# Hybrid decoder step on one core: who copies turned pages and probabilities, where swish stands, and the order of loads in the output projection

## The reference, cut to what matters

```
z = rmsnorm(x) @ w_in                       # q, k, v, indexer q and k, conv inputs
attention: each query attends to its top 256 keys by an indexer's score
   prompt: causal over 1024 rows; sample: 2048 cached rows (16 pages) + 8 new ones
convolution branch: GLU -> depthwise conv (31) -> layernorm -> c * sigmoid(c)
m = concat(attention, conv) @ w_out ;  x = x + rmsnorm(m)
x = x + rmsnorm( relu(rmsnorm(x) @ w_up)^2 @ w_down )
```

## Time and profile before

| | us |
|---|---|
| median of 3 runs | 1666.31 |
| lowest, highest | 1664.51, 1667.41 |
| the profiled execution | 1657.09 |
| its span | 1655.3 |
| TensorE busy in the span | 1534.6 (93%) |
| VectorE, ScalarE, GpSimd busy | 692.7, 605.1, 434.5 |

### The profile page before, as it was taken

One profiled execution on the slowest core, in us unless ns is written; L12 is line 12 of the kernel. 1 busy time (PEld: TensorE's weight loads), 2 busy tenths in 40 slices (PEclk: granted clock), 3 DMA queues, 4 the chain that ended last, 5 costly groups with the idle time before them and its releaser, 6 DMA issues.

```text
span 1655.3 us, 22168 instructions
## 1 busy us (share of the span) xinstructions
PE 1534.6 (93%) x8544; PEld 1278.0 (77%) x8544; DVE 692.7 (42%) x1318; ACT 605.1 (37%) x1084; POOL 434.5 (26%) x445
## 2 busy tenths in 40 slices
PE   4798898998969999888999999999999999999995
PEld 2356625663468877456879999999999999999995
DVE  1234916788977545243554222222222222222234
ACT  3112725988425764474443121121212112130211
POOL 2132100112595321341433121212121212122224
PEclk8999998999989998998999999999999999999998
DMA  6010104142106100544001111111111111111112
GB/s 209 20 36 24 52 2 128 60 69 55 19 1 185 54 2 1 216 166 147 0 1 55 48 39 51 38 51 39 50 38 51 38 51 38 51 38 51 39 49 98
DMA packets 92884, 97.66 MB, mean 59 GB/s; under 512 B 14822, under 2 KB 80438, under 8 KB 90500
## 3 DMA queue, kind: packets, MB, share of 16 engines
q1 hardware_dynamic: 89324, 75.71, 15.8%
q0 software_dynamic: 3488, 20.98, 3.4%
HBM read 85.55 MB, written 11.45 MB: 59 GB/s over the span
## 4 chain that ended last, share of the span: by engine, by line
PE 51%; DMA 1%; POOL 1%; DVE 1%; issue 0%; SPq 0%; ACT 0%; DVEq 0%; POOLq 0%; ACTq 0%
PE ps L2237 17%; PE ps L2239 17%; PE ps L2238 17%; DMA wraw<-in_w_up 1%; PE ps L2272 0%; POOL wlo L2098 0%; POOL y L2133 0%; DVE y L2406 0%; DMA out_y_p<-y 0%; DMA moT<-in_g_mix_post 0%; SPq L2050 0%; PE ps L2324 0%; DVE y L2416 0%; ACT whi L2147 0%; DVE moT L2359 0%
## 5 line engine op out<-in xcount | busy, mean ns | idle before, releaser
L2098 POOL TENSOR_TENSOR wlo<-wraw,whi 128x1024 fp32r<-128x1024 f32 x62 | 149.1, 2405 | 591.9 <-ACT whi L2147 591.9
L2238 PE MATMUL ps<-xlo,whi 128*128 128x384 f32 (+1 forms) x768 | 250.3, 326 | 0.0
L2237 PE MATMUL ps<-hhi,whi 128*128 128x384 f32 (+1 forms) x720 | 235.1, 327 | 0.8 <-POOL wlo L2098 0.8
L2239 PE MATMUL ps<-hhi,wlo 128*128 128x384 f32 (+1 forms) x720 | 235.2, 327 | 0.0
L2238 PE MATMUL ps<-hlo,whi 128*128 128x384 f32 (+1 forms) x720 | 234.9, 326 | 0.0
L2147 ACT CAST whi<-wraw 128x1024 fp32r<-128x1024 f32 x62 | 65.1, 1050 | 302.1 <-PE ps L2239 293.8
L2383 DVE TENSOR_TENSOR rel<-rel 128x384 f32<-128x384 f32 (+1 forms) x96 | 51.5, 537 | 283.7 <-ACT rel L2212 283.7
L2238 PEld LDWEIGHTS ps<-xlo,whi 128*128 128x128 f32 x768 | 144.2, 188 | 0.0
L2212 ACT ACTIVATE rel<-ps 128x384 f32<-128x384 f32 (+1 forms) x96 | 45.4, 474 | 264.3 <-PE ps L2239 264.3
L2237 PEld LDWEIGHTS ps<-hhi,whi 128*128 128x128 f32 x720 | 135.2, 188 | 1.1 <-POOL wlo L2098 1.1
L2239 PEld LDWEIGHTS ps<-hhi,wlo 128*128 128x128 f32 x720 | 135.1, 188 | 0.0
(11 more groups left out here) (306 smaller groups left out, 2854.7 us busy)
## 6 DMA issues: line engine op xcount, KB each, us to landing
wraw<-in_w_up SPq DMA_DIRECT2D x32, 512.0 KB, 4.1
wraw<-in_w_down SPq DMA_DIRECT2D x32, 512.0 KB, 3.4
x<-in_x SPq DMA_DIRECT2D x16, 512.0 KB, 5.6
w<-in_w_rows SPq DMA_DIRECT2D x2, 2048.0 KB, 10.6
w<-in_w_u SPq DMA_DIRECT2D x2, 2048.0 KB, 10.6
wo_raw<-in_w_out SPq DMA_DIRECT2D x8, 512.0 KB, 3.9
out_y_p<-y SPq DMA_DIRECT2D x8, 512.0 KB, 2.6
up<-by_channel SPq DMA_DIRECT2D x32, 86.0 KB, 4.2
```

Source lines behind the costliest of these rows:

```text
L2098: nc.gpsimd.tensor_tensor(wlo_of(j, last), raw[:], whi_of(j, last), ALU.subtract).then_inc(s_wlo, 1)
L2237: nc.tensor.matmul(o, wh, xh, start=first, stop=False)
L2238: nc.tensor.matmul(o, wh, xl, start=False, stop=False)
L2239: return nc.tensor.matmul(o, wl, xh, start=False, stop=last)
```

## The change

In the sample stage the copies of turned pages and of turned probabilities are shared out by two lists, each copy with the semaphore of its engine; in turns 8 to 11 pages are ScalarE's, 12 to 15 VectorE's, elsewhere they alternate. ScalarE's exponentials of pair 0 come after all page copies of its share for pairs 0 and 1. `swish(k)` follows the probability copies of k directly, and `swish_product(k)` too, ahead of the maximum of k+1. In the projection SyncE issues w_up unit 0 first, then seven x loads, waits for `s_cl`, and issues the gain and the last two x loads; unit 1 follows when unit 0 is split. ScalarE and VectorE make the attention parts of tile s+2 first in turn s, VectorE waits for the gain after them; unit 0 of w_up is copied after the squares of tile 0 and split after its inverse root.

```diff
+    PAGE_BY = ["act" if (PT <= e < PT + 4 or e % 2 == 0) and not PT + 4 <= e < 2 * PT else "dve"
+               for e in range(PT * NPAIR)]
+    PROB_BY = ["act" if q % 2 == 0 else "dve" for _ in range(NPAIR) for q in range(SP_TURNS)]
...
@@ ScalarE, sample stage
+            def take_pages(e0, e1):
+                for e in range(e0, e1):
+                    if PAGE_BY[e] == "act":
+                        act.wait_ge(s_kt, e + 1)
+                        b, q = e // (NPG // 4), e % (NPG // 4)
+                        if b >= 2:
+                            act.wait_ge(s_ss, b // 2)
+                        nc.scalar.copy(kpT[:, b % 2, q * 512:(q + 1) * 512], bank[5 + e % 2]).then_inc(s_ke["act"], 1)
+            def take_probabilities(k):
...
             act.wait_ge(s_t, len(turns))
-            for e in range(PT + 2):
-                take_pages(e)
+            take_pages(0, 2 * PT)
             exponentials(0)
-            for e in range(PT + 2, 2 * PT):
-                take_pages(e)
...
             for k in range(NPAIR):
+                take_probabilities(k)
+                if k < len(TCH):
+                    swish(k)
                 if k == 2:
                     attn_high(0)
                     attn_high(1)
                 if k + 1 < NPAIR:
                     exponentials(k + 1)
                 if k + 2 < NPAIR:
-                    for e in range(PT * (k + 2), PT * (k + 3)):
-                        take_pages(e)
-                if k < len(TCH):
-                    swish(k)
+                    take_pages(PT * (k + 2), PT * (k + 3))
@@ TensorE, sample stage
                     if e >= 2:
-                        pe.wait_ge(s_ke, e - 1)
-                    if e % PT < 2 and pr >= 2:
-                        pe.wait_ge(s_se, SP_TURNS * (pr - 1))
+                        pe.wait_ge(s_ke[PAGE_BY[e - 2]], taken(PAGE_BY, e - 2, PAGE_BY[e - 2]))
+                    if e % PT == 0 and pr >= 2:
+                        probabilities_taken(SP_TURNS * (pr - 1) - 1)
...
@@ VectorE, sample stage
+            dve.wait_ge(s_t, len(turns))
+            take_pages(0, 2)
             dve.wait_ge(s_z, 1)
...
-            maximum(0)
-            for k in range(NPAIR):
...
+            take_pages(2, PT)
+            maximum(0)
+            take_pages(PT, 2 * PT)
+            for k in range(NPAIR):
+                take_probabilities(k)
+                if k < len(TCH):
+                    swish_product(k)
                 if k == 2:
                     attn_low(0)
                     attn_low(1)
                 if k + 1 < NPAIR:
                     maximum(k + 1)
-                if k >= 1:
-                    swish_product(k - 1)
...
+                if k + 2 < NPAIR:
+                    take_pages(PT * (k + 2), PT * (k + 2) + PT // 2)
                 dve.wait_ge(s_sa, k + 1)
...
+                if k + 2 < NPAIR:
+                    take_pages(PT * (k + 2) + PT // 2, PT * (k + 3))
@@ projection, SyncE
-            for i in range(RT):
+            load(wraw0, s_raw[0], up[:, :, 0:P], P)
+            for i in range(RT - 2):
+                sp.dma_start(x2[:, i, :], a["x"][i * P:(i + 1) * P, :]).then_inc(s_x, 16)
+            sp.wait_ge(s_cl, RT)
+            sp.dma_start(gpost, a["g_mix_post"]).then_inc(s_g, 16)
+            for i in range(RT - 2, RT):
                 r = rows_of(i)
                 sp.dma_start(x2[0:r, i, :], a["x"][i * P:i * P + r, :]).then_inc(s_x, 16)
-            load(wraw0, s_raw[0], up[:, :, 0:P], P)
             sp.wait_ge(s_wlo, 1)
             load(wraw0, s_raw[0], up[:, :, P:2 * P], P)
-            sp.wait_ge(s_cl, RT)
-            sp.dma_start(gpost, a["g_mix_post"]).then_inc(s_g, 16)
@@ projection, GpSimd
-            low(0, 0, None)
             for s in range(RT):
                 inverse_rms(s, 0, s_q, s_r)
+                if s == 0:
+                    low(0, 0, None)
@@ projection, ScalarE
-            high(0, 0, None)
...
                     act.wait_ge(s_o, s + 1)
+                    if s + 2 < RT:
+                        attn_high(s + 2)
...
-                    if s + 2 < RT:
-                        attn_high(s + 2)
+                if s == 0:
+                    high(0, 0, None)
@@ projection, VectorE
-            dve.wait_ge(s_g, 16)
...
                 if s < RT:
                     r = rows_of(s)
+                    if s + 2 < RT:
+                        attn_low(s + 2)
+                    if s == 0:
+                        dve.wait_ge(s_g, 16)
                     dve.wait_ge(s_r, s + 1)
...
-                    if s + 2 < RT:
-                        attn_low(s + 2)
```

More of the change, by code:

```diff
@@ L1288, in phase_attend @@
     s_kt = sem("a_kt")
-    s_ke = sem("a_ke")
+    s_ke = {"act": sem("a_ke"), "dve": sem("a_kd")}
     s_ss = sem("a_ss")
@@ L1293, in phase_attend @@
     s_st = sem("a_st")
-    s_se = sem("a_se")
+    s_se = {"act": sem("a_se"), "dve": sem("a_sd")}
     s_so = sem("a_so")
@@ L1343, in phase_attend, with taken @@
     PT = 2 * NPG // 4
+    PAGE_BY = ["act" if (PT <= e < PT + 4 or e % 2 == 0) and not PT + 4 <= e < 2 * PT else "dve"
+               for e in range(PT * NPAIR)]
+    PROB_BY = ["act" if q % 2 == 0 else "dve" for _ in range(NPAIR) for q in range(SP_TURNS)]
+    def taken(by, e, who):
+        return by[:e + 1].count(who)
     ln_tiles = [[i for i in range(RT) if t0 <= i * P < t0 + w] for t0, w in TCH]
@@ L1520, in _ @@
                     squares(ln_step(j, 3))
[L1523 to L1528, removed]
+            def take_pages(e0, e1):
[7 more added lines that the diff above has]
+            def take_probabilities(k):
+                if k >= 1:
+                    act.wait_ge(s_so, k)
+                else:
+                    act.wait_ge(s_o, NHD // NKV)
+                for q in range(SP_TURNS):
+                    e = SP_TURNS * k + q
+                    if PROB_BY[e] == "act":
+                        act.wait_ge(s_st, e + 1)
+                        nj = min(4, NPG + 1 - 4 * q)
+                        w = P if nj > 1 else NT
+                        nc.scalar.copy(probST[0:w, 4 * q:4 * q + nj, :],
+                                       bank[5 + e % 2].rearrange("p (b t) -> p b t", t=P)[0:w, 0:nj, :]
+                                       ).then_inc(s_se["act"], 1)
             def swish(n):
@@ L1673, in _, with pages_taken, probabilities_taken @@
                     widen((j - WIDE) // NH)
+            def pages_taken(e):
+                for who in ("act", "dve"):
+                    if taken(PAGE_BY, e, who):
+                        pe.wait_ge(s_ke[who], taken(PAGE_BY, e, who))
+            def probabilities_taken(e):
+                for who in ("act", "dve"):
+                    if taken(PROB_BY, e, who):
+                        pe.wait_ge(s_se[who], taken(PROB_BY, e, who))
             def turn_pages(pr, half):
@@ L1691, in pair_scores @@
             def pair_scores(pr):
-                pe.wait_ge(s_ke, PT * (pr + 1))
+                pages_taken(PT * (pr + 1) - 1)
                 if pr >= 1:
@@ L1713, in turn_probabilities @@
                     if e >= 2:
-                        pe.wait_ge(s_se, e - 1)
+                        pe.wait_ge(s_se[PROB_BY[e - 2]], taken(PROB_BY, e - 2, PROB_BY[e - 2]))
                     for j in range(4 * q, min(4 * q + 4, NPG + 1)):
@@ L1841, in _, with take_pages @@
                     place(j // NH - 1)
+            def take_pages(e0, e1):
+                for e in range(e0, e1):
+                    if PAGE_BY[e] == "dve":
+                        dve.wait_ge(s_kt, e + 1)
+                        b, q = e // (NPG // 4), e % (NPG // 4)
+                        if b >= 2:
+                            dve.wait_ge(s_ss, b // 2)
+                        nc.vector.tensor_copy(kpT[:, b % 2, q * 512:(q + 1) * 512], bank[5 + e % 2]
+                                              ).then_inc(s_ke["dve"], 1)
+            dve.wait_ge(s_t, len(turns))
+            take_pages(0, 2)
             dve.wait_ge(s_z, 1)
@@ L1868, in maximum, with take_probabilities @@
                                         AX_X, ALU.max, negate=True).then_inc(s_sm, 1)
-            maximum(0)
-            for k in range(NPAIR):
+            def take_probabilities(k):
+                if k >= 1:
+                    dve.wait_ge(s_so, k)
+                else:
+                    dve.wait_ge(s_o, NHD // NKV)
                 for q in range(SP_TURNS):
                     e = SP_TURNS * k + q
[L1874 to L1883, removed]
+                    if PROB_BY[e] == "dve":
+                        dve.wait_ge(s_st, e + 1)
+                        nc.vector.tensor_copy(probST[:, 4 * q:4 * q + 4, :],
+                                              bank[5 + e % 2].rearrange("p (b t) -> p b t", t=P)
+                                              ).then_inc(s_se["dve"], 1)
+            take_pages(2, PT)
[5 more added lines that the diff above has]
+                    swish_product(k)
                 if k == 2:
```

8 lines of the change are left out of this document (4 added, 4 removed).

## The result

| | before | after |
|---|---|---|
| median (4 runs each), us | 1666.17 | 1650.06 |
| lowest, highest | 1664.51, 1667.41 | 1648.29, 1654.57 |
| profiled execution, and its span | 1657.09, 1655.3 | 1649.70, 1647.8 |

The ratio is 0.9908, with a 95% interval of 0.9886 to 0.993: 16.1 us less. The forecast was 1661.6 and its range ended at 1657.5, so the prediction was wrong in size. But the two profiled executions are only 7.5 us apart, and the changed stretch of their traces holds 5.2 of it. Most of this document is about that gap.

What follows compares the result with a forecast made beforehand. TensorE's matmuls were taken to bound half the span, with waits in the changed stretch. Terms 8.0 + 3.0 + 0.2 − 0.1 − 1.5 − 1.5 − 1.8 = 6.3, less a 1.6 clock fall, gave 4.7 gained: 1661.6 us, range 1657.5 to 1666.3.

Steps and rivals of the forecast that it cites:

- Projection: Output projection: reordered loads and copies remove tile 2's wait of 4.97 us and its slow clock; 8.0 us gained.
- Head: Start of the sample stage: pair 0's probability turns start 3.0 us sooner; VectorE's page copies lose at most 0.1.
- Pairs 0 and 1: Sample stage: earlier swish delays the maximum to 10.2 us after the pair's probability turns start; 1.5 us lost each.
- the probability copies: Sample stage: sharing them between ScalarE and VectorE gains only in pair 3, by 0.2 us.
- the shared page copies: Sample stage: VectorE's share of page evictions gives nothing back in pairs 0 and 1; its last adds 0.1 us.
- Pair 2: Sample stage: swish and attention halves delay the maximum to 11.0 us after probability turns start; 1.8 us lost.
- Pair 3: End of sample stage: 0.2 us gained from shared probability copies; a clock fall behind pair 2 costs 1.6.
- rival A: The forecast itself: one added clock fall, gain 4.7 us, 1661.6; chance 0.43.
- B: Sample stage: no added clock fall, gain 6.3 us, 1660.0; chance 0.26.
- C: Sample stage: a clock fall in each of three pairs, gain 1.5 us, 1664.8; chance 0.18.
- D: Sample stage: GpSimd holds up VectorE's last product and maximum in three pairs, 8.5 us slower, 1674.8; chance 0.06.
- E: Sample stage: dear table switches end the three swishes 3.9 us later in all, gain 2.4, 1663.9; chance 0.07.

Runs made afterwards that it cites:

- before_again: The kernel before, unchanged, timed against itself on one chip: median 1664.10 us, ratio to before 1.0005 (12 runs).
- after_again: The changed kernel, unchanged, timed again against the kernel before: median 1657.16 us, ratio 0.9976 (12 runs).
- filled: Useless matmuls added to the layernorm's row squares in both kernels: before 1660.80 us, changed 1653.90 us.
- proj_only: The kernel before with only the changed output projection: median 1653.37 us, ratio to before 0.9936 (9 runs).
- sample_only: The kernel before with only the changed sample stage: median 1665.45 us, ratio to before 1.0017 (12 runs).
- swish_only: The kernel before with only swish and its product at their new places, all copies as before: 1667.03 us (one run).
- product_late: The changed kernel with VectorE's swish product and two low halves behind the next maximum: 1657.09 us, ratio to before 0.9968 (12 runs).
- loads_only: The kernel before with only SyncE's new load order in the projection: 1654.67 us (one run).
- four_pages: The changed kernel with probability copies on VectorE, swish in its old place, only page turns 12 to 15 on VectorE: 1648.89 us, ratio to before 0.9898.
- fill_after: The changed kernel with useless matmuls added to the layernorm's row squares: median 1653.90 us, ratio to before 0.9943 (6 runs).

## Why the prediction was wrong

The failed step is the one of a single sentence: "The median of the runs is 1666.31, 9.2 above; I add the same difference to that." It took the distance from the profiled execution to the median for a constant and the 2.9 us of three runs for the spread. On the record of the later runs it is the distance between two ways in which the same code runs, at 1.2 GHz from about 652 to 680 us or not: 11.1 us between before_again and the first trace of before. For the changed kernel the distance was 0.4 (1650.06 less 1649.70). Executions of one kernel differ by 11 to 15 us; the range was 8.8 wide. The real worth of the change came out at 4.0 us (after_again), 6.9 (filled) and 5.2 (the two first traces), with 4.7 forecast; the first measurement's 16.1 is beyond all of them. Why its four runs of the changed kernel lay at 1648 to 1655 and those of before at 1664 to 1667 was not found. The mean granted clock of those four changed runs was 0.973 to 0.975; of the 12 runs of after_again only one had more than 0.971 (0.977, 1649.82 us). So they look like runs without the long fall. But on the chip of after_again both kernels had short and long executions, with 5 of 32 of before below 1658. Chance, the chip or a tie to the changed code stay open; the third is weakened by before_again and proj_only showing the low clock in identical code, but not excluded.

The terms, against the first two traces:

- *Projection, 8.0 forecast, 9.79 measured* (114.17 less 104.38). Hole and slow tile went as forecast: tile 2 followed tile 1 at 775.5 and took 10.9; the w_up load landed in 4.3 and the gain by 769.2 (768.5 forecast, and the stage began 2.3 later). proj_only shows the missing 1.7: its 106.03 has the low clock at the start (0.64 over its first 4 us), 104.38 has not. In the kernel before that fall cost nothing, as the hole's end was set by the loads: sample_only, without it, has a hole of 6.77 and 113.81. Without the hole it counts. I had it in the range only.
- *Head, 3.0 less 0.1 forecast, 2.09 measured.* VectorE's page copy takes 0.69, not the 0.65 of half of a merged row; the first scores came 0.4 later, and turn 8 waited 0.35 for keys. The keys of run 3 did not limit.
- *Pairs 0 and 1, 1.5 each forecast, 1.37 and 1.39 measured.* The maximum at T+9.98 (10.2 forecast). Size and course are right by the trace: the table load came at T+3.27, behind ScalarE's copy, which I had ending at T+3.4. But I put the whole loss to swish and gave the probability copies a gain of 0.2. swish_only has swish in line too and loses nothing in pair 1, because its table load hides; ScalarE's probability copies ahead of it are worth 0.8. And the shared page copies, which I put at 0.1, cost 0.54 where the maximum is not late.
- *Pair 2, 1.8 forecast, 1.57 measured.* The maximum at T+10.78 (11.0 forecast).
- *Pair 3, 0.2 gained and a fall of 1.6 forecast, 2.34 lost.* The fall came behind pair 2, as rival A said, and cost most of it in the value products.
- *Rivals.* B and C did not occur in the trace: one fall came in pair 3, none in pairs 0 and 1. D was real but without effect in this change: two products took 2.23 beside GpSimd, where 1.1 is due, and the last ones were free. E did not occur: 1.30 from load to activation again, so against the drain that the Trainium skill adds ("ScalarE: Activation LUTs", section "What ACT_TABLE_LOAD costs"). Rival E's gain of 2.4 also left out the fall that A counts; with it the gain was 0.8.

The sum of the measured terms is 9.79 + 2.09 − 1.37 − 1.39 − 1.57 − 2.34 = 5.2. That it is so near to 4.7 is luck in part: the projection gave 1.8 more than forecast, the head 0.8 less, pair 3 lost 0.9 more.

## What to carry to other kernels

Before a median is forecast, compare the profiled execution's time with the runs; a distance beyond the runs' own spread (9.2 against 2.9 us here) can mean two ways of running, and the effect is to be read from stages cut at fixed points of the trace. In these traces a table load was hidden where nothing of its engine stood between it and the wait for the new work; a cheap copy put there moved it onto the path. Sharing out copies is not free where the first engine was not late (0.54 us a pair here): share only where one is.

## What was not expected of the hardware

- The granted clock fell at 650 to 655 us in every profiled execution without filling. It came back before 658 in four of them and only at 676 to 682 in nine; in before_again TensorE was busy in 23.8 of the 25 us from 655 to 680. The same code does both.
- In four of the five traces in which the clock fell before or in pair 3, it did not fall again at the start of the projection: 2.3 us lost and 1.7 given back in the kernel after. The fifth, product_late, had both falls, and loads_only, four_pages and fill_after neither; loads_only and proj_only differ in this with the same code ahead of it.
- With filling matmuls in the wait of 1.15 us and between those of one column the clock stayed at 1.00 over 655 to 680 in all five filled traces.
